# Sums of squares over a head: one fp32 product replaced by two fp32r products of a high and a low part

## The reference, cut to what matters

```python
def _l2norm(x):
    return x * lax.rsqrt(jnp.sum(x * x, axis=-1, keepdims=True) + NORM_EPS)
# in _gated_deltanet
q = _l2norm(q.reshape(b_, s_, B_HEADS, HEAD_DIM)) * (HEAD_DIM ** -0.5)
k = _l2norm(k.reshape(b_, s_, B_HEADS, HEAD_DIM))
...
_, o = lax.scan(_delta_step, state0, xs)
o = _rmsnorm(o, norm_g) * jax.nn.silu(zf)     # mean of squares over the 64 of a head
```

## Time and profile before

| What | us |
|---|---|
| Median of 3 runs (lowest, highest) | 2361.18 (2361.14, 2362.14) |
| The profiled execution's own time | 2358.52 |
| Its span, from the first to the last instruction | 2356.9 |
| TensorE busy in it | 2327.5 |
| VectorE busy | 1271.7 |
| ScalarE busy | 844.0 |
| Mean granted clock of TensorE | 0.996 of full |

### The profile page before, as it was taken

The page is one execution under the profiler, slowest core; times in us unless marked ns, Lnnn a source line. Parts: engine busy times, 40 slices in busy tenths (PEclk is TensorE's granted clock), DMA queues, the critical chain, the costliest instruction groups (busy, mean ns, idle before and its releaser), DMA issues.

```text
span 2356.9 us, 36519 instructions
## 1 busy us (share of the span) xinstructions
PE 2327.5 (99%) x14038; PEld 1885.0 (80%) x14038; DVE 1271.7 (54%) x1777; ACT 844.0 (36%) x1243; POOL 113.7 (5%) x220
## 2 busy tenths in 40 slices
PE   8999999999999999999999999999999999999998
PEld 6888888777777888888878888877777788888886
DVE  4554556675457664433465545567645576443334
ACT  5231334532355442223342223345225555331232
POOL 1010000020000000000000001001000000000000
PEclk9999999999999999999999999999999999999999
DMA  8564563243234334423245645623332352443231
GB/s 327 188 214 143 181 217 121 82 136 100 82 120 143 117 133 147 148 98 102 94 143 186 206 143 187 216 90 108 100 104 86 114 177 82 159 159 110 89 111 58
DMA packets 95151, 325.28 MB, mean 138 GB/s; under 512 B 12904, under 2 KB 13576, under 8 KB 94016
## 3 DMA queue, kind: packets, MB, share of 16 engines
q1 hardware_dynamic: 57456, 216.09, 27.7%
q0 software_dynamic: 23760, 82.48, 11.0%
q10 hardware_dynamic: 13824, 25.17, 3.1%
HBM read 306.34 MB, written 14.73 MB: 136 GB/s over the span
## 4 chain that ended last, share of the span: by engine, by line
PE 90%; DVE 4%; DMA 2%; ACT 2%; issue 1%; ACTq 0%; SPq 0%; POOL 0%; DVEq 0%; POOLq 0%
PE PS L524 81%; PE PS L792 2%; PE PS L1046 1%; DMA ada<-in_ada_first_dram 1%; DVE up_m L1981 1%; DMA gb<-g_rows 1%; DVE wl L1479 0%; ACTq L1372 0%; PE PS L1020 0%; PE PS L784 0%; ACT g_in L1406 0%; DVE up_m L1984 0%; PE PS L716 0%; PE PS L980 0%; PE PS L1029 0%
## 5 line engine op out<-in xcount | busy, mean ns | idle before, releaser
L1479 DVE TENSOR_TENSOR wl<-raw,wh 128x1024 fp32r<-128x1024 f32 (+2 forms) x360 | 466.1, 1295 | 786.5 <-ACT wh L1111 786.1
L524 PE MATMUL PS<-uh,wh 128*128 128x512 f32 x2192 | 873.4, 398 | 4.7 <-DVE wl L1479 2.6
L524 PE MATMUL PS<-ul,wh 128*128 128x512 f32 x2192 | 855.8, 390 | 0.0
L524 PE MATMUL PS<-uh,wl 128*128 128x512 f32 x2192 | 855.6, 390 | 0.0
L1111 ACT ACTIVATE wh<-raw 128x1024 fp32r<-128x1024 f32 (+2 forms) x360 | 401.6, 1115 | 889.3 <-PE PS L524 874.9
L524 PEld LDWEIGHTS PS<-uh,wh 128*128 128x128 f32 x2192 | 412.1, 188 | 104.5 <-issue 9.0
L524 PEld LDWEIGHTS PS<-uh,wl 128*128 128x128 f32 x2192 | 412.3, 188 | 87.8
L524 PEld LDWEIGHTS PS<-ul,wh 128*128 128x128 f32 x2192 | 412.4, 188 | 82.8 <-issue 1.9
L524 PE MATMUL PS<-hh,wh 128*128 128x512 f32 x736 | 286.9, 390 | 0.0
L524 PE MATMUL PS<-hl,wh 128*128 128x512 f32 x736 | 286.4, 389 | 0.0
L524 PE MATMUL PS<-hh,wl 128*128 128x512 f32 x736 | 286.3, 389 | 0.0
(11 more groups left out here) (271 smaller groups left out, 1593.6 us busy)
## 6 DMA issues: line engine op xcount, KB each, us to landing
raw<-in_ffn_in_dram SPq DMA_DIRECT2D x176, 512.0 KB, 3.5
ada_raw<-in_ada_w_dram POOLq DMA_DIRECT2D x144, 512.0 KB, 3.8
raw<-in_mix_in_dram SPq DMA_DIRECT2D x88, 512.0 KB, 3.5
raw<-in_ffn_out_dram SPq DMA_DIRECT2D x32, 768.0 KB, 4.5
raw<-in_ffn_out_dram SPq DMA_DIRECT2D x32, 640.0 KB, 4.0
g_in<-gates_dram ACTq DMA_DIRECT2D x48, 256.0 KB, 3.1
ada<-in_ada_first_dram SPq DMA_DIRECT2D x8, 1024.0 KB, 16.3
raw<-in_mix_up_dram SPq DMA_DIRECT2D x16, 512.0 KB, 3.9
```

What stands on the lines that cost most here:

```text
L524: mm = e.matmul(PS[:, bank, :], w[:, j % 2, k * P:(k + 1) * P], v[:, k, :], start=(k == 0 and w is wh and v is xh), stop=(k == K - 1 and w ...
L1479: TTo(wl[:, j % 2, 0:K * P], raw[:, j, 0:K * P], wh[:, j % 2, 0:K * P], ALU.subtract)\
```

## The change

Each sum of squares by one fp32 matmul becomes two fp32r matmuls into the same PSUM bank. ScalarE copies the squares to `sq_hi` in fp32r, VectorE writes `sq - sq_hi` to `sq_lo` in fp32r, and the block of ones is copied once to `same_r` in fp32r. The squares, the roots and all that follows are unchanged, and so is the fp32 use of `same_chunk` in line 737. `sq_hi` and `sq_lo` lie over space that is free in both stages. On TensorE the wait for the squares becomes one for the low part. On ScalarE the high copy of tile i follows its square in step m = 8+i, behind a wait for that square, and the outputs' two high copies follow their two squares ahead of `gate_step(16)`. On VectorE the subtraction of tile i comes in step m = 8+i behind `ahead(MIX + m)`, and the outputs' two come between `ahead` of gate units 15 and 16.

```diff
@@ -130,6 +130,7 @@
         pick = place("pick", [P, 2 * HALF], F32)
         tri = place("tri", [P, P], F32)
         same_chunk = place("same_chunk", [P, P], F32)
+        same_r = place("same_r", [P, P], F32R)
 
         tri_c = place("tri_c", [P, CHUNK], F32)
         later_c = place("later_c", [P, CHUNK], F32)
@@ -182,6 +183,8 @@
         Ym = [None] + [place(f"Ym{v}", [P, 8, CHUNK], F32, at)
                        for v, at in enumerate((A0 + 30720, A0 + 4096, A0 + 6144, W0 + 28672, W0 + 30720), 1)]
         cT = place("cT", [P, 8, CHUNK], F32, A0 + 20480)
+        sq_hi = place("sq_hi", [P, 2, SEQ], F32R, A0 + 20480)
+        sq_lo = place("sq_lo", [P, 2, SEQ], F32R, A0 + 26624)
         eg = place("eg", [P, 2, SEQ], F32, A0 + 12288)
         bb = place("bb", [P, 2 * 8 * CHUNK], F32, A0)
 
@@ -268,7 +271,10 @@
         conv_done = sig("conv_done", 6)
         conv_silu = sig("conv_silu", 6)
         conv_step = sig("conv_step", 18)
+        same_ready = sig("same_ready")
         l2_sq = sig("l2_sq", 4)
+        l2_hi = sig("l2_hi", 4)
+        l2_lo = sig("l2_lo", 4)
         l2_mm = sig("l2_mm", 4)
         l2_root = sig("l2_root", 4)
         l2_inv = sig("l2_inv", 4)
@@ -311,6 +317,8 @@
         o_mm = sig("o_mm", 1)
         o_done = sig("o_done", 1)
         on_sq = sig("on_sq", 2)
+        on_hi = sig("on_hi", 2)
+        on_lo = sig("on_lo", 2)
         on_mm = sig("on_mm", 2)
         on_root = sig("on_root", 2)
         on_step = sig("on_step", 6)
@@ -737,10 +745,12 @@
                         e.matmul(PS[:, 6, 48:64], same_chunk[:, :], sc[:, 0:16], start=True, stop=True)\
                             .then_inc(gc_mm.sem, 1)
 
-                    e.wait_ge(l2_sq.sem, l2_sq.at(l, i + 1))
+                    e.wait_ge(same_ready.sem, 1)
+                    e.wait_ge(l2_lo.sem, l2_lo.at(l, i + 1))
                     if i >= 2:
                         e.wait_ge(l2_root.sem, l2_root.at(l, i - 1))
-                    e.matmul(PS[:, 4 + i % 2, :], same_chunk[:, :], sq[:, i % 2, :], start=True, stop=True)\
+                    e.matmul(PS[:, 4 + i % 2, :], same_r[:, :], sq_hi[:, i % 2, :], start=True, stop=False)
+                    e.matmul(PS[:, 4 + i % 2, :], same_r[:, :], sq_lo[:, i % 2, :], start=False, stop=True)\
                         .then_inc(l2_mm.sem, 1)
                 proj(13)
                 gates(2)
@@ -945,8 +955,9 @@
                 e.wait_ge(st_done.sem, st_done.at(l, NCH))
                 for i in range(2):
 
-                    e.wait_ge(on_sq.sem, on_sq.at(l, i + 1))
-                    e.matmul(PS[:, 4 + i, :], same_chunk[:, :], sq[:, i, :], start=True, stop=True)\
+                    e.wait_ge(on_lo.sem, on_lo.at(l, i + 1))
+                    e.matmul(PS[:, 4 + i, :], same_r[:, :], sq_hi[:, i, :], start=True, stop=False)
+                    e.matmul(PS[:, 4 + i, :], same_r[:, :], sq_lo[:, i, :], start=False, stop=True)\
                         .then_inc(on_mm.sem, 1)
                 for t in range(TT):
                     mm = e.transpose(PS[:, 6, t * P:(t + 1) * P], ct[5][:, t * P:(t + 1) * P], ident[:, :])
@@ -1270,6 +1281,11 @@
                         if i >= 2:
                             e.wait_ge(l2_mm.sem, l2_mm.at(l, i - 1))
                         e.activation(sq[:, i % 2, :], bp[:, i, :], ACT.Square).then_inc(l2_sq.sem, 1)
+                        if l == 0 and i == 0:
+                            e.wait_ge(tables_in.sem, 16 * 10)
+                            e.activation(same_r[:, :], same_chunk[:, :], ACT.Copy).then_inc(same_ready.sem, 1)
+                        e.wait_ge(l2_sq.sem, l2_sq.at(l, i + 1))
+                        e.activation(sq_hi[:, i % 2, :], sq[:, i % 2, :], ACT.Copy).then_inc(l2_hi.sem, 1)
                     if 9 <= m <= 12:
                         i = m - 9
                         if i >= 2:
@@ -1315,6 +1331,9 @@
                 e.wait_ge(o_done.sem, o_done.at(l, 1))
                 for i in range(2):
                     e.activation(sq[:, i, :], bp[:, 4 + i, :], ACT.Square).then_inc(on_sq.sem, 1)
+                for i in range(2):
+                    e.wait_ge(on_sq.sem, on_sq.at(l, i + 1))
+                    e.activation(sq_hi[:, i, :], sq[:, i, :], ACT.Copy).then_inc(on_hi.sem, 1)
                 gate_step(16)
                 for i in range(2):
                     e.wait_ge(on_mm.sem, on_mm.at(l, i + 1))
@@ -1694,6 +1713,12 @@
                         ahead(MIX + m + 2)
                     elif m >= 8:
                         ahead(MIX + m)
+                    if 8 <= m <= 11:
+                        i = m - 8
+                        if i >= 2:
+                            e.wait_ge(l2_mm.sem, l2_mm.at(l, i - 1))
+                        e.wait_ge(l2_hi.sem, l2_hi.at(l, i + 1))
+                        TTo(sq_lo[:, i % 2, :], sq[:, i % 2, :], sq_hi[:, i % 2, :], ALU.subtract).then_inc(l2_lo.sem, 1)
                     if m < 6:
 
                         e.wait_ge(in_done.sem, in_done.at(l, m + 1))
@@ -1856,6 +1881,9 @@
                     if n % 2 == 0:
                         ahead(MIX + gate_unit(11 + n // 2))
                 ahead(MIX + gate_unit(15))
+                for i in range(2):
+                    e.wait_ge(on_hi.sem, on_hi.at(l, i + 1))
+                    TTo(sq_lo[:, i, :], sq[:, i, :], sq_hi[:, i, :], ALU.subtract).then_inc(on_lo.sem, 1)
                 ahead(MIX + gate_unit(16))
 
                 def normalised(i):
```

## The result

| | before | after |
|---|---|---|
| Median, us (lowest to highest, runs, same chip) | 2359.86 (2357.03 to 2364.56, 18) | 2365.90 (2361.71 to 2369.30, 18) |
| Ratio after / before, 95% interval | | 1.0021 [1.0013, 1.0028] |
| The profiled execution's own time | 2358.52 | 2362.47 |
| Its span | 2356.9 | 2360.8 |
| Mean granted clock in it | 0.996 | 0.995 |

A forecast was written before the change was run, and what follows sets the result against it. TensorE bounds the kernel, but the decays' rows' trip nearly ties with it before the key products. A layer: 0.8 (`gb`) + 1.4 (clock) - 0.8 (outputs) = +1.4; two, +2.8 on 2361.18: 2364.0 us, range 2359.8 to 2366.4.

The forecast's parts named there:

- The sum: TensorE, both stages: two fp32r matmuls take 0.46 us where one fp32 sum takes 0.86, saving 0.40 a sum.
- The saving is swallowed at the key products: Line 766: TensorE already waits 0.2 us, so the 1.62 us saved before it only lengthens the wait.
- ScalarE 0.5 us later at the row copies: Query and key stage: three high copies, partly absorbed by idle time, make line 1288's row copies 0.5 us late.
- The rows' trip: GpSimd's DMAs out and back: a colliding weight load adds 0.3 us (-0.3 to 1.3), so `gb` lands 0.8 later.
- rival C: Weight load and `h_rows` collide fully, 1.3 us a layer, with the clock's full 1.7: +5.4, 2366.6 us; chance 0.15.
- VectorE late, but hidden: VectorE reaches line 1662 some 1.1 us later, hidden under its wait for `gb`, with 0.9 to spare.
- The pause: Before line 766: TensorE stands idle for 0.2 + 1.6 + 0.8 = 2.6 us.
- The clock: Behind the idle time at line 766 the clock falls to 1.2 GHz, costing 1.4 us a layer (0 to 1.7).
- Outputs: Outputs stage: the sums save 0.81 us a layer on TensorE; copies and subtractions add nothing, with 1.1 us of cover.
- Rival A: The clock holds at line 766: 2361.2 us, 2360.6 with the trip unharmed, 2362.6 with one layer's fall; chance 0.25.
- B: TensorE's whole saving counts, the rows' trip being off the path: -4.9 us, 2356.3 us; chance 0.04.
- D: Outputs stage: low parts come late, so its 0.8 us gain goes: +1.6, 2365.6 us; chance 0.04.

The follow-up runs named there:

- burden: Kernel before plus the change's high copies and subtractions for queries and keys, sums kept in fp32, outputs stage old; 2365.01 us, ratio 1.0025.
- null: The kernel before, unchanged, measured again against itself; 2358.25 us, ratio 0.9997.
- late_load: Changed kernel with SyncE holding the loads of weight unit 16 and later until the decays' rows are written out; 2360.10 us, ratio 1.0007 to the kernel before.
- qk_only: Kernel before with the change in the query and key stage alone, outputs summed in fp32 as before; 2364.31 us, ratio 1.0029.
- fill: Changed kernel with 14 unused fp32r products on TensorE in the pause before the key products; 2360.81 us, ratio 1.0009 to the kernel before.
- swap2: Changed kernel, VectorE's last reciprocal moved ahead of its wait for `gb`, ScalarE's unit 13 scaling ahead of the first decays' exponential; 2352.03 us, 0.9975 to before.
- swap2_out: The two moves of swap2 made on out_only; 2357.38 us, ratio 0.9994 to the kernel before.
- out_only: Kernel before with the change in the outputs stage alone, queries and keys summed in fp32 as before; 2360.88 us, ratio 1.0009.
- out_again: The kernel out_only, run again; 2360.09 us, ratio 1.0004 to the kernel before.

## Why the prediction was right, and where it was off

The forecast was slower by 2.8 us; the ratio gives 5.0. The direction and each step of the route held; the size was low. Step by step:

- **The sum.** Forecast 0.46 in place of 0.86 us. Two starts lie 0.24 and 0.24 apart, 0.48; what lies behind a sum comes 0.37 to 0.44 us earlier. Right.
- **The saving is swallowed at the key products.** Right: burden, which lacks it, takes as long. But "TensorE waits 0.2 us there now" was one draw; null shows 1.06 and 0.85, and the mean of the eight layers is 0.6.
- **ScalarE 0.5 us later at the row copies.** Counted from the first sum, which nothing of the change can move, the row copies start after 10.28 us in the changed kernel (469.39 - 459.11) and 10.27 in burden, against 9.70 in the kernel before and 9.69 in null: 0.6 later. The size is nearly right, but the working does not give it. With 0.64 a copy, 1.28 - 0.89 leaves 0.39, and 0.39 + 0.64 - 0.35 is 0.7; the 0.1 of overlap, added once more, makes 0.8.
- **The rows' trip**, "bounds from -0.3 to 1.3, I take 0.3". This is the mis-sized term. `h_rows` and `gb` together took 10.85 and 10.88 us against 9.59 and 9.83 in the given profile: +1.26 and +1.05, nearly rival C's price. Against the mean of the eight layers with the old stage (10.1, of 9.6 to 10.7) it is 0.7. The write alone is 1.2 us longer than in late_load, which shows that the load does it, and 1.0 longer than the mean of those eight. I had taken the net difference between the two layers of before for the size, which was a draw.
- **VectorE late, but hidden.** It still stands idle for 2.18 us before line 1681, which it reaches 0.9 us later after the first sum than before (forecast 1.1). Right where the trip is long; in qk_only's second layer, with the short trip, VectorE came last.
- **The pause**, forecast 2.6 = 0.2 + 1.6 + 0.8, was 3.4 = 0.6 + 1.55 + 1.3. The 0.6 is the mean wait of the old order and the 1.3 are 0.6 of ScalarE and 0.7 of the trip. Of the miss of 0.8, half is the draw of the starting wait, which costs no time, and half the trip.
- **The clock**, forecast 1.4 a layer "nearest to the case of line 723": 1.62 and 1.49 where it fell. It did in 5 of the 8 layers in which the profiles of after, burden, qk_only and late_load had a pause over 1.4 us. fill shows its price in time.
- **Outputs**, forecast -0.81 without idle time: -0.78 twice, none. The low parts are ready at 631.16 and wanted at 632.51, a cover of 1.3 us.

With the measured terms a layer has 1.3 (key products later, from first sum to first key product 31.7 against 30.5 in the mean of the eight) + 1.55 - 0.78 = +2.1, 4.2 in both where the clock falls each time, which lies within 3.1 to 6.6. With a fall in only 5 of 8 layers it would be 2.9, just below. The mean granted clock over all runs, 0.9964 before and 0.9948 after, speaks for a fall in most of them: the difference is 3.8 us of 2360. Rival A fell on the median, though qk_only's best run is what it describes. B is out: it needed the trip off the path, and swap2 shows that kernel. C had the right mechanism and, for the given pair, nearly the right price of the trip. D is out. By the ratios late_load (the trip) and fill (the clock) each take back over half of the loss; they overlap, since the clock held in one layer of late_load's profile, so part of what it took back is the clock's. The forecast gave slower by more than 0.2% a chance of 0.18, and 0.21% is what came. So some luck is in it: the range ends 5.2 us above its starting median, the ratio gives 5.0, the medians of the pair 6.0, and the new median fell inside the range also because the kernel before came out 1.3 us lower than the three runs that the forecast started from.

What stays open: whether the outputs stage's 0.8 us a layer reaches the time. Three kernels were expected to show it, and none did. swap2_out leaves it possible; out_only and out_again speak against it, with intervals that begin above 0.9993. For it speak the traces, and qk_only, which lacks the saving and came out 1.9 us slower than the changed kernel by the ratios, within an uncertainty larger than that.

## What to carry to other kernels

A saving on the busiest engine is worth nothing where another route ends at the same time: first look at how much the two routes differ, over more than one execution, and change the order of the in-order engines that hold the other route. Here the same edit cost 5 us in the given order and brought 5 with two moved blocks. Work added to a feeding engine moves every transfer whose buffer it frees; ask beside what those will then run. A pause on TensorE can cost twice: here 3.4 us of idle time brought another 1.5 to 1.6 us behind it where the clock fell.

## What the runs showed of the hardware

- With fourteen needless products in a pause of 3.4 us the clock stayed at 2.4 GHz and the time was 2.8 us lower by the ratios (intervals overlap by 0.0005).
- The clock's fall is a draw: behind the same line of the same program (line 723) it fell in both layers of one profile and in neither of another, about 1.6 us each; behind the key products it held after 3.20 us of idle time (qk_only) and fell after 1.85 (burden).
- A weight load on SyncE's queue, issued 1.4 us before a small write on GpSimd's, lengthened the write from 3.0 to 4.2 us; in 1 of 14 layers it did not (2.75).
- The trip of the same rows out to memory and back took 9.6 to 10.7 us over eight layers of kernels that are alike in that stage.
